# Opening a gated feed-forward by input chunk: eight gate and up blocks accumulate at once in a two-block transformer kernel

## The reference, cut to what matters

```python
mods = (jax.nn.silu(c) @ w_ada[l] + b_ada[l]).reshape(B, N_MOD, D_MODEL)   # 9 rows of 1024
n = modulate(rmsnorm(h, g_pre[l, 0]), shift(0), scale(0))                  # x * (1 + scale) + shift
f = (jax.nn.silu(n @ w_gate) * (n @ w_up)) @ w_down                        # D_FF = 2816
h = h + 0.5 * gate(0) * rmsnorm(f, g_post[l, 0])
```

## Time and profile before

| | |
|---|---|
| median of 3 runs | 1234.78 us (1233.88 to 1236.3) |
| the profiled execution | 1232.68 us |
| its span, first to last instruction | 1231.4 us |
| granted TensorE clock, mean share of full | 0.985 |
| ScalarE busy | 616.5 us (50%) |
| GpSimd busy | 57.5 us (5%) |
| moved by DMA | 231.78 MB, mean 188 GB/s |

### The profile page before, as it was taken

How to read it: one execution, slowest core, us unless ns; L and a number is a source line. 1 busy time by engine, 2 the same in 40 slices (tenths; PEclk the granted TensorE clock), 3 DMA queues, 4 the chain that set the end, 5 groups by cost and what they waited for, 6 DMA issues and landing times.

```text
span 1231.4 us, 19574 instructions
## 1 busy us (share of the span) xinstructions
PE 1164.0 (95%) x7742; PEld 1068.7 (87%) x7742; DVE 803.9 (65%) x1335; ACT 616.5 (50%) x1096; POOL 57.5 (5%) x75
## 2 busy tenths in 40 slices
PE   1899999999988999999999899999999889999998
PEld 1799999989987999999989888999998778899997
DVE  6888877668654665655558876555567665655554
ACT  4444444545653644444555555454546445545453
POOL 4000000000000000000002110000000000000000
PEclk8899999999997999999999999999999999999999
DMA  9999888443322275565443223554544514455540
GB/s 379 352 395 357 321 315 317 150 173 135 104 104 69 100 260 208 215 227 190 154 152 127 103 104 137 179 198 175 201 173 152 188 35 154 171 194 183 192 151 35
DMA packets 34011, 231.78 MB, mean 188 GB/s; under 512 B 3704, under 2 KB 5120, under 8 KB 6528
## 3 DMA queue, kind: packets, MB, share of 16 engines
q1 hardware_dynamic: 31952, 226.24, 50.2%
q10 hardware_dynamic: 1968, 4.29, 1.0%
HBM read 229.45 MB, written 1.06 MB: 187 GB/s over the span
## 4 chain that ended last, share of the span: by engine, by line
PE 78%; DVE 13%; ACT 5%; issue 2%; POOL 1%; DMA 1%; DVEq 0%; SPq 0%; ACTq 0%; POOLq 0%
PE ps L375 38%; PE pacc L375 35%; DVE wlo L338 3%; ACT wk L972 2%; DVE raw L316 2%; ACT whi L337 1%; PE ps L388 1%; POOL st L482 1%; DVE st L967 1%; PE ps L385 1%; PE pacc L514 1%; PE ps L514 1%; DVE tmp L651 1%; DVE arena L1229 1%; DMA cst<-in_const 1%
## 5 line engine op out<-in xcount | busy, mean ns | idle before, releaser
L338 DVE TENSOR_TENSOR wlo<-raw,whi 128x1024 fp32r<-128x1024 f32 x353 | 430.0, 1224 | 184.5 <-ACT whi L337 178.9
L337 ACT ACTIVATE whi<-raw 128x1024 fp32r<-128x1024 f32 x353 | 369.0, 1054 | 154.3 <-PE pacc L375 80.8
L375 PE MATMUL ps<-nhi,whi 128*128 128x256 f32 x1384 | 399.5, 289 | 20.5 <-DVE wlo L338 17.8
L375 PE MATMUL ps<-nhi,wlo 128*128 128x256 f32 x1384 | 392.8, 284 | 0.0
L375 PE MATMUL ps<-nlo,whi 128*128 128x256 f32 x1384 | 392.7, 284 | 0.0
L375 PEld LDWEIGHTS ps<-nhi,whi 128*128 128x128 f32 x1384 | 266.4, 192 | 27.3 <-ACT whi L337 19.3
L375 PEld LDWEIGHTS ps<-nlo,whi 128*128 128x128 f32 x1384 | 266.5, 193 | 5.1 <-issue 1.0
L375 PEld LDWEIGHTS ps<-nhi,wlo 128*128 128x128 f32 x1384 | 266.3, 192 | 0.0
L375 PE MATMUL pacc<-whi,hhi 128*128 128x512 f32 x444 | 174.7, 393 | 1.1 <-ACT sg L718 1.1
L375 PE MATMUL pacc<-wlo,hhi 128*128 128x512 f32 x444 | 174.0, 392 | 0.0
L375 PE MATMUL pacc<-whi,hlo 128*128 128x512 f32 x444 | 172.8, 389 | 0.0
(11 more groups left out here) (280 smaller groups left out, 1348.1 us busy)
## 6 DMA issues: line engine op xcount, KB each, us to landing
raw<-in_stream SPq DMA_DIRECT2D x213, 1024.0 KB, 4.9
gates<-in_g_post ACTq DMA_DIRECT2D x3, 512.0 KB, 13.3
h<-in_x SPq DMA_DIRECT2D x1, 1024.0 KB, 7.1
cst<-in_const ACTq DMA_DIRECT2D x1, 1024.0 KB, 9.3
arena<-bias_rows ACTq DMA_DIRECT2D x1, 1024.0 KB, 16.2
out<-tmp SPq DMA_DIRECT2D x4, 256.0 KB, 2.1
silu_c<-in_c_row ACTq DMA_DIRECT2D x1, 512.0 KB, 5.8
arena<-in_final_g SPq DMA_DIRECT2D x1, 512.0 KB, 5.7
```

What stands on the lines that cost most here:

```text
L337: t_hi = act.do(lambda e: e.activation(whi[:, s, :], src, ACT.Copy), arrived, room)
L338: t_lo = dve.do(lambda e: e.tensor_tensor(wlo[:, s, :], src, whi[:, s, :].bitcast(F32), ALU.subtract), arrived, room, t_hi)
L375: return e.matmul(o, lt[a], rh[b], start=start and first, stop=stop and last)
```

## The change

It makes ten edits.

- A function `ffn_steps` lists the pairs (gate and up of a block) and downs of a feed-forward in order; with `made` blocks done already, two downs go ahead of each pair until the downs have caught up.
- The stream gives, for each chunk k, the ada units of rows 0 and 1 and then two new units, `ffn0_fg` and `ffn0_fu`: rows 128k to 128k+127 of the gate and the up matrix, columns 0 to 1023, which are blocks 0 to 7.
- The opening loop, once chunk k is modulated, issues 48 matmuls: for eight blocks and for gate and up the three products of chunk k. All eight banks are held, block j in bank j, gate in its left and up in its right half. In the last chunk block after block is closed and given to `hidden`.
- There are eight slots for hidden blocks in the first feed-forward (hhi, mhi and new tiles xhi, xlo) and five in the others.
- Shift and scale columns of the opening, and the two diagonals, are made by ScalarE; the factor in them that doesn't depend on `c` is made ahead on VectorE (`gain`).
- Ada units of rows 2 to 5 (32) are spread over the 50 weights left of the first feed-forward (factor 1.1), those of rows 6 and 7 (16) over in_t units 10 to 19 and out units 0 to 3 (factor 1.2).
- `extra` is called after every pair and every down.
- A differential head starts only when its rotated keys are three steps old.
- After the last pair `hold` is set as before, and the last two downs note when their hidden slots come free.
- The tile `st` has 400 columns in place of 480.

The diff, cut to its core:

```diff
+def ffn_steps(blocks, made=0):
+    steps, n = [], 0
+    for j in range(made, blocks):
+        for _ in range(2):
+            if n < j - 1:
+                steps.append(("down", n))
+                n += 1
+        steps.append(("pair", j))
+    return steps + [("down", j) for j in range(n, blocks)]
...
-    ffn0 = spread(ffn("ffn0_", DFF // P, ("gate", "up")), (2, 3, 4, 5, 6, 7), 1.03)
-    plan = [("ada", 0), ("ada", 1)] * 6 + ffn0[0:2] + [("ada", 0), ("ada", 1)] * 2 + ffn0[2:]
+    plan = []
+    for k in range(8):
+        plan += [("ada", 0), ("ada", 1), ("ffn0_fg", k), ("ffn0_fu", k)]
+    plan += spread(ffn("ffn0_", DFF // P, ("gate", "up"), 8), (2, 3, 4, 5), 1.1)
     plan += [("in_v", k) for k in range(8)] + [("in_i", 0)]
-    plan += [("in_t", j) for j in IN_ORDER]
-    plan += [("out", k) for k in OUT_ORDER]
+    plan += [("in_t", j) for j in IN_ORDER[0:10]]
+    plan += spread([("in_t", j) for j in IN_ORDER[10:]] + [("out", k) for k in OUT_ORDER[0:4]], (6, 7), 1.2)
+    plan += [("out", k) for k in OUT_ORDER[4:]]
...
+        hslots = [(hhi[:, n, :], hlo[:, n, :]) for n in range(2)] + [(mhi[:, n, :], mlo[:, n, :]) for n in range(3)]
+        hslots += [(xhi[:, n, :], xlo[:, n, :]) for n in range(3)]
+        hid = {"work": 0, "ring": 8, "free": {n: [] for n in range(8)}}
...
-            ts.append([diagonal(i, r, t, t_const)])
+            ts.append([act.do(lambda e: e.activation(dg[:, i, :], ident, ACT.Copy, scale=r), t, t_const)])
+        gain = mod[:, 40:48]
+        g_pre, b_scale = (cl[:, COLS[n] + a:COLS[n] + a + 8] for n, a in (("g_pre", 0), ("b_ada", 8)))
+        t_gain = dve.do(lambda e: e.scalar_tensor_tensor(gain, b_scale, 1.0, g_pre, ALU.add, ALU.mult), t_cols)
...
+        held = fix + [banks.take() for _ in range(4)]
+        made = []
         for k in range(8):
-            feed(2 * k + 2 if k < 6 else 2 * k + 4)
-            t_shift = ada_columns(0, sh[0], k)
-            t_scale = scale_columns(1, sc[0], COLS["g_pre"], k)
...
+            feed(4 * k + 2)
+            t_shift = act.do(lambda e: e.activation(sh[0][:, k:k + 1], adac[:, k:k + 1], ACT.Identity,
+                                                    bias=col("b_ada", k)), ada["done"][0, k], t_cols)
+            t_scale = act.do(lambda e: e.activation(sc[0][:, k:k + 1], adac[:, 8 + k:9 + k], ACT.Identity,
+                                                    bias=gain[:, k:k + 1], scale=col("g_pre", k)),
+                             ada["done"][1, k], t_gain)
+            for _ in shifted_chunk(k, zs[k], n1, sc[0][:, k:k + 1], sh[0][:, k:k + 1], t_shift, t_scale, by_act=True):
+                pass
+            feed(4 * k + 4)
+            units = [Unit(("ffn0_fg", k)), Unit(("ffn0_fu", k))]
+            for j, n in ([(j, n) for n in range(2) for j in range(8)] if k < 7 else
+                         [(j, n) for j in range(8) for n in range(2)]):
+                b, u = held[j], units[n]
+                w, o = u.part(j * P, (j + 1) * P), b.ap[:, n * T:(n + 1) * T]
+                pe.wait(u.ready, b.free if k == 0 else [], n1.t[k])
+                x = n1.rows(k)
+                put(o, w[0], x[0], k == 0 and n == 0)
+                put(o, w[1], x[0])
...
+                if k == 7 and n == 1:
+                    made.append(hidden(j, b.ap[:, 0:T], b.ap[:, T:2 * T], (b,), tk))
...
-        done = feed_forward("ffn0_", DFF // P, True, n1, during_ffn0)
+        done = feed_forward("ffn0_", DFF // P, True, n1, during_ffn0, made)
...
-            side.add(diff_head(hh), lambda hh=hh: ripe(hh, 8 + hh))
+            side.add(diff_head(hh), lambda hh=hh: ripe(hh, 8 + hh) and side.now - born[8 + hh] >= 3)
```

More of the change, by code:

```diff
@@ L247, in build @@
         gates = sb("gates", [P, 2, D], stack=early)
+        xhi = sb("xhi", [P, 3, T], F32R, early)
+        xlo = sb("xlo", [P, 3, T], F32R, early)
         psum = [ctx.enter_context(nc.psum_tensor(f"ps{b}", [P, 512], F32)) for b in range(4, 8)]
@@ L742, in first_two, with feed_forward @@
             return held, toks
-        def feed_forward(name, blocks, gated, parts, extra=None):
-            prev, following = None, None
-            hp = Parts(hhi, hlo)
-            for j in range(blocks + 1):
-                if j == 0:
+        def feed_forward(name, blocks, gated, parts, extra=None, made=()):
+            now = dict(enumerate(made))
+            hid["ring"] = 8 if made else 5
+            steps = ffn_steps(blocks, len(made))
+            for what, j in steps[:-2]:
+                if what == "down":
+                    ps, pt = now[j]
+                    u = Unit((name + "down", j))
+                    done = []
+                    for i in range(2):
+                        outs = [(fix[2 * i + f].ap, [(hidden_tokens(ps, i), u.part(f * 512, f * 512 + 512), pt)],
+                                 j == 0, False) for f in range(2)]
+                        after = list(u.ready)
+                        if j == 0:
+                            after += fix[2 * i].free + fix[2 * i + 1].free
+                        done.append([products([o], after) for o in outs])
+                    u.release(done[1][1])
+                    hid["free"][ps] = [done[1][1]]
+                    feed()
+                elif j == 0:
                     (b0, b1), (t0, t1) = first_two([(name + "gate", 0), (name + "up", 0)] if gated else
@@ L764, in feed_forward @@
                         u.release(tk)
-                    now = (hidden(b.ap[:, 0:T], b.ap[:, T:2 * T], (b,), tk) if gated else
-                           hidden(None, b.ap[:, 0:T], (b,), tk))
+                    now[j] = (hidden(j, b.ap[:, 0:T], b.ap[:, T:2 * T], (b,), tk) if gated else
+                              hidden(j, None, b.ap[:, 0:T], (b,), tk))
                     feed()
-                if j == blocks - 1:
-                    before, prev = prev, now
-                    hold.append(j)
-                    if extra is not None:
-                        extra()
-                    continue
-                if j == blocks:
-                    return last_two([Unit((name + "down", n)) for n in (blocks - 2, blocks - 1)],
-                                    [([hp.tokens(q, i) for i in range(2)], t) for q, t in (before, prev)])
-                if prev is not None:
-                    ps, pt = prev
-                    u = Unit((name + "down", j - 1))
-                    done = []
-                    for i in range(2):
-                        outs = [(fix[2 * i + f].ap, [(hp.tokens(ps, i), u.part(f * 512, f * 512 + 512), pt)],
-                                 j == 1, False) for f in range(2)]
-                        after = list(u.ready)
-                        if j == 1:
-                            after += fix[2 * i].free + fix[2 * i + 1].free
-                        done.append([products([o], after) for o in outs])
-                    u.release(done[1][1])
-                    hid["free"][ps] = [done[1][1]]
-                    feed()
-                prev = now
+                    if j == blocks - 1:
+                        hold.append(j)
                 if extra is not None:
                     extra()
+            ends = last_two([Unit((name + "down", n)) for n in (blocks - 2, blocks - 1)],
+                            [([hidden_tokens(now[n][0], i) for i in range(2)], now[n][1])
+                             for n in (blocks - 2, blocks - 1)])
+            for n in (blocks - 2, blocks - 1):
+                hid["free"][now[n][0]] = [ends[1][1]]
+            return ends
         n1 = Parts(nhi, nlo)
@@ L1547, in lay_out @@
         src[f"mlp{f}_down"] = v["w_down_2"][f].reshape(-1, P, D)
+    for u in ("gate", "up"):
+        src[f"ffn0_f{u[0]}"] = np.ascontiguousarray(v[f"w_ffn_{u}"][0, 0][:, 0:1024]).reshape(8, P, 1024)
     w = v["w_in"][0]
```

66 lines of the change are left out of this document (34 added, 32 removed).

## The result

The changed kernel takes 1242.45 us in the median (1241.24 to 1242.77), the kernel before 1234.96 in the runs beside it: ratio 1.0058, 95% interval [1.0041, 1.0076]. On another chip the same file gave 1.0084 [1.0066, 1.0102]. It is slower by 0.6 to 0.8%, where 0.2% faster was forecast; 1242.45 also lies above the range's end of 1240. The profiled execution took 1242.77 (span 1240.7, against 1231.4).

The account below looks back on a forecast made before the run. TensorE's late start bounded the opening, the chain through VectorE and ScalarE the heads' stage, nearly balanced with TensorE; -16.7 + 14.5 + 0 = -2.2 us against the 1234.78 median gave 1232.6 us, range 1219 to 1240.

Parts of the forecast that it names:

- Part 1, the opening: First feed-forward: starting blocks 0 to 7 chunk by chunk, paced by TensorE, gains 16.7 us, ends 10 and 19.
- the third rival: Opening: VectorE and ScalarE set the pace, 6.5 us a chunk, 6 us of gain lost, 1238.6 us; chance 0.10.
- Start: Opening: TensorE's first feed-forward matmul at 20.5 us, from copies ending at 16.93 plus columns, modulation, nhi and first splits.
- The tail: End of the opening's eight blocks: closing them through silu, product, copy and residue makes TensorE 1.5 us late, ends 0 and 5.
- Part 2, the reductions: Heads' stage: 16 reductions of modulations 6 and 7 on VectorE's queue cost 14.5 us, upper end 18.2 without the clock.
- The three reductions taken as free: Behind in_t blocks 18 and 19: TensorE carries the chain and VectorE's gaps take them, 0; without that cover 3.4 us.
- a rival of 0.16: Heads' stage: added waits lower TensorE's clock, 3.8 us more, all 16 reductions on the path, 5.3 slower, 1240 us; chance 0.16.
- The 4.7 us: Time after the last matmul of the opening's turn at which TensorE's clock fell, used as the threshold for single waits.
- The absorbed rival: Heads' stage: VectorE's idle 19.2 us absorb the reductions, 1221 us, or Part 3 brings up to 8, 1224; chance 0.36 together.
- Part 3, the heads: Differential heads: starting a head one step later taken as 0, ends 11 us faster and 1.4 us slower.
- Part 4: Hidden slots, extra steps after every unit and diagonals on ScalarE: 0, or 1 us if the diagonals' cover is gone.
- The slow rival: Heads' stage: reductions cost 18.2 us and the lowered TensorE clock 3.8 more, 5.3 us slower, 1240 us; chance 0.16.

Follow-up runs that it names:

- the run with both rows back: The changed kernel with the reductions of modulation rows 6 and 7 spread over the first feed-forward again: 1227.68 us, ratio 0.9957 to the kernel before.

## Why the prediction was wrong

It put the change at -2.2 us; the profiled executions differ by +10.1, the spans by 9.3, and the stages add up to +9.2. That is 11.4 us from the forecast, in four parts: the opening brought 3.2 less, the reductions cost 3.4 more, the heads 3.3 more, and the clock at the index keys, which wasn't in the sum, 1.5.

- **Part 1, the opening: right in kind, too high.** TensorE paces it from the first chunk, and the third rival falls. 13.5 gained instead of 16.7, inside its ends. Start 22.30 for 20.5 (1.8): the turn ended later (1.4 at the copies' end), which is a difference between executions and could as well have gone the other way; the two columns took 0.7 for 0.4, hand-overs the rest. Clock 2.4 for 1.9 (0.5). The tail was 1.1 for 1.5 (-0.4), and 0.3 was idle time between chunks. The rest (1.0) was in the base: TensorE is busy 193.9 us from 22.30 to the end, 195.7 with the 1.8 that moved and 193.3 with the clock loss taken off, and 20.5 + 193.3 + 1.9 + 1.5 is 217.2, not the 216.2 that a gain of 16.7 means.
- **Part 2, the reductions: the step that failed is the sum's clock.** The block-by-block reading of the chain gave 14.5 us of waiting, and 13.6 of idle time were measured (12.3 if the run with both rows back is the base), with 1.7 of longer busy time that goes with the waits. The three reductions taken as free were free. But I had made the clock a rival of 0.16 with a price of 3.8, on the ground that single waits stay under 4.7 us. It came too, for 2.6 in this pair, with waits of 3.27 and 3.38. The two weren't alternatives: 14.5 of waiting left room for a clock loss on top. Of the 3.4 us missing, 2.6 are this clock and 0.8 the waits (15.3 for 14.5); 14.5 + 3.8 would have been 18.3 against 17.9.
- **The 4.7 us were no guide.** They came from one profile, and its row gives 4.6. In fourteen other profiles the clock fell in the same pause of the opening 2.0 to 4.6 us after the turn, in four only after work had resumed, and in one, with a pause of 3.3 us, not at all. The return to the full level, read as 3.9 us after work resumed, is 4.1 in the row.
- **The absorbed rival (0.36) was my largest error of weight.** The stage's length was 150.7 with the reductions alone added. VectorE's idle 19.2 us were of no use: it waits for ScalarE in 18.4 of them. By the Trainium skill (Perfetto Trace Analysis, Identifying the Most-Contended Engine) VectorE wasn't the engine to mind in this stretch, busy 68%; the trace disagrees, 18 us for work on the less busy engine. Behind the value and first in_t units the same work is free, and there the Trainium skill's rule holds.
- **Part 3, the heads: taken 0, it costs 3.3** (2.7 to 3.5 in the runs), outside the upper end of 1.4. The step that failed is "whose order changes and whose sum doesn't", where I looked at the period alone. The period did stay. A row of eight heads in step also has a beginning and an end: it starts 3.8 us later, and the last two heads closing up gives back only part.
- **Part 4** held for the diagonals: made on VectorE again, they changed nothing that can be told. What I hadn't in the sum at all was the clock at the index keys, 1.5 us in this pair of profiles.
- **Two slips** that don't move the forecast: the chance of "slower by more" is 0.04 and 0.27 of the three rivals, 0.31 less a little, not 0.21. And of the 12 reductions made before the first feed-forward matmul only eight start after the turn has ended.

With the measured terms: -13.5 + 1.5 + 17.9 + 3.3 = +9.2. The slow rival had the right sign and the right two causes in the heads' stage, and its 1240 is near by luck too: it had all 16 reductions on the path where 12 were, and neither the heads nor the smaller opening.

Open: why the clock loss in the heads' stage varies between executions with nearly the same waits. Open too is whether the 7.5 us between the medians are less than the 9.3 between the profiles because before's profile had a full clock at the index keys where its other executions had not. Two profiles speak for it: both runs that keep the old opening have the fall, and take 9.7 us there for 8.2.

## What to carry to other kernels

Before putting side work "beside" a busy TensorE, follow the chain through that stretch: if it runs through an engine's in-order queue, the work costs about its full length there, however idle that engine looks, and it can be free a few units earlier. Add the clock as a range on top of the price of the waits, in place of weighing it against them. Don't take one profile's turn of the clock for a rule. When a pipelined row of tasks is started later, price the start and the tail, since an unchanged period hides both.

## What the hardware showed unexpectedly

- TensorE's granted clock fell to its lower level (0.50) while the engine was busy without a gap, in or within 0.6 us after a row of 48 matmuls of 72 columns, in 15 of 16 profiles, and stayed full in 4 of 4 when the row was cut in two by 24 matmuls of 256 columns.
- In the heads' stage it fell 2.8 us into a wait of 3.3 us, and 1.0 us after another of 3.4. In the opening it fell 2.0 to 4.6 us into the pause in fifteen profiles, and in one with a pause of 3.3 us it didn't fall.
- The same 32 matmuls of the turn took 5.25 us in one profile and 6.48 in another, without a gap in either; that alone moved the start of the feed-forward by as much as the edits to it did.
- The same GpSimd instruction on 128x1 numbers took 1.54 us in all eleven profiles with the diagonals on ScalarE, where it starts beside a 128x1024 reduction of VectorE (12.41 and 12.32 here), and 0.55 in all nine others. Why wasn't tested.

```profile
12.41 1.54 POOL L496 TENSOR_TENSOR st<-st,mod 128x1 f32<-128x1 f32 x1 [1.74 <-DVE mod L830]
```
